# Column sums of the modulation vectors: block turning on VectorE and one small product, in place of eight turns or eight products on TensorE

## What is computed

```python
def _modulation(cvec, w, b):
    m = jax.nn.silu(cvec) @ w + b          # cvec: 2048, w: 2048 x 6144
    return m[..., :D_MODEL], m[..., D_MODEL:2 * D_MODEL], m[..., 2 * D_MODEL:]   # shift, scale, gate
```

## Time and profile before

| | us |
|---|---|
| median of three runs | 2005.06 |
| lowest, highest | 2004.21, 2007.96 |
| span of the profiled execution | 2003.6 |
| TensorE busy, matmuls | 1967.3 (98%), 12638 instructions |
| VectorE busy | 1612.0 (80%), 2209 instructions |
| ScalarE busy | 967.3 (48%) |
| GpSimd busy | 211.4 (11%) |
| HBM read | 430.83 MB |
| granted TensorE clock, mean | 0.995 of full |

### The profile page before, as it was taken

One profiled execution on the slowest core, in us unless ns is written; L12 is line 12 of the kernel. 1 busy time (PEld: TensorE's weight loads), 2 busy tenths in 40 slices (PEclk: granted clock), 3 DMA queues, 4 the chain that ended last, 5 costly groups with the idle time before them and its releaser, 6 DMA issues.

```text
span 2003.6 us, 35002 instructions
## 1 busy us (share of the span) xinstructions
PE 1967.3 (98%) x12638; PEld 1767.2 (88%) x12638; DVE 1612.0 (80%) x2209; ACT 967.3 (48%) x1457; POOL 211.4 (11%) x294
## 2 busy tenths in 40 slices
PE   7999999999999999999999999999999998999997
PEld 7998899899888888888888899887888888999986
DVE  6996677757888998889999878779987877678754
ACT  6553446645444344443444455236565455554453
POOL 0000000011000220001311111111000131000011
PEclk9999999999999999999999999999999999999999
DMA  6554454346777787777888874677657884568553
GB/s 239 168 159 137 159 198 127 106 158 200 231 234 229 265 317 238 237 235 241 286 295 295 305 262 159 228 232 230 211 169 226 273 285 156 193 196 288 189 190 126
DMA packets 121148, 434.43 MB, mean 217 GB/s; under 512 B 13248, under 2 KB 15680, under 8 KB 120784
## 3 DMA queue, kind: packets, MB, share of 16 engines
q1 hardware_dynamic: 92240, 328.11, 49.8%
q0 software_dynamic: 28800, 104.87, 15.8%
HBM read 430.83 MB, written 2.10 MB: 216 GB/s over the span
## 4 chain that ended last, share of the span: by engine, by line
PE 85%; DVE 9%; DMA 3%; issue 2%; ACT 1%; SPq 0%; DVEq 0%; POOL 0%; POOLq 0%; ACTq 0%
PE ps L649 33%; PE ps L650 16%; PE ps L636 7%; PE ps L637 7%; PE ps L638 7%; DVE w_lo L1690 3%; PE ps L784 2%; DMA side<-w_side 2%; PE ps L1108 1%; PE ps L1098 1%; PE ps L717 1%; PE ps L719 1%; PE ps L718 1%; DVE mod_sum L1707 1%; PE ps L826 1%
## 5 line engine op out<-in xcount | busy, mean ns | idle before, releaser
L649 PE MATMUL ps<-ba_act,w_hi 128*128 128x512 f32 x3264 | 1152.4, 398 | 2.6 <-DVE w_lo L1690 2.6
L650 PE MATMUL ps<-ba_act,w_lo 128*128 128x256 f32 x3264 | 910.8, 279 | 0.0
L1690 DVE TENSOR_TENSOR w_lo<-raw,w_hi 128x1024 fp32r<-128x1024 f32 x610 | 728.9, 1236 | 35.1 <-ACT w_hi L1252 34.2
L649 PEld LDWEIGHTS ps<-ba_act,w_hi 128*128 128x128 f32 x3264 | 612.6, 188 | 149.4 <-issue 4.2
L1252 ACT ACTIVATE w_hi<-raw 128x1024 fp32r<-128x1024 f32 x610 | 612.4, 1042 | 222.0 <-PE ps L638 162.1
L650 PEld LDWEIGHTS ps<-ba_act,w_lo 128*128 128x128 f32 x3264 | 615.1, 188 | 1.3 <-issue 1.2
L636 PE MATMUL ps<-ba_act,w_hi 128*128 128x256 f32 x912 | 261.8, 287 | 5.2 <-DVE w_lo L1690 5.1
L637 PE MATMUL ps<-ba_act,w_hi 128*128 128x256 f32 x912 | 258.9, 284 | 0.0
L638 PE MATMUL ps<-ba_act,w_lo 128*128 128x256 f32 x912 | 258.8, 284 | 0.0
L1707 DVE SCALAR_TENSOR_TENSOR mod_sum<-side,csil,mod_sum 128x1024 f32<-128x1024 f32 x180 | 229.0, 1286 | 32.1 <-DMA side<-w_side 28.9
L544 POOL DMA_DIRECT2D side<-w_side x200 | 108.1, 541 | 1350.8 <-DVE mod_sum L1707 770.9
(11 more groups left out here) (368 smaller groups left out, 1860.4 us busy)
## 6 DMA issues: line engine op xcount, KB each, us to landing
raw<-w_main SPq DMA_DIRECT2D x610, 512.0 KB, 4.4
side<-w_side POOLq DMA_DIRECT2D x200, 512.0 KB, 4.6
x_tok<-x_in SPq DMA_DIRECT2D x4, 512.0 KB, 8.0
ctx_tok<-ctx_tok SPq DMA_DIRECT2D x1, 2048.0 KB, 10.6
y_out<-res SPq DMA_DIRECT2D x4, 384.0 KB, 3.1
table<-counts_tab SPq DMA_DIRECT2D x1, 512.0 KB, 12.9
y_out<-res SPq DMA_DIRECT2D x2, 256.0 KB, 3.0
cons<-cons_in SPq DMA_DIRECT2D x1, 478.0 KB, 10.7
```

What stands on the lines that cost most here:

```text
L649: pe.matmul(ps[:, bank, :], wh, act[:, kt, :, :], start=first and b == 0, stop=False)
L650: mm = pe.matmul(ps[:, bank, 0:T], wl, act[:, kt, 0, :], start=False, stop=last and b == 7)
L1690: dve.tensor_tensor(w_lo[:, slot, 0:n], raw[:, slot, 0:n], w_hi[:, slot, 0:n].bitcast(F32), ALU.subtract)\
```

## The change

Of eleven groups (all but `ev_out`) the sum over the partitions is split in two.

- VectorE turns the whole 128 x 1024 sum in one instruction that transposes 32 x 32 blocks, each inside its own 32 partitions and 32 columns, and then adds up each block's 32 columns (`turn_mods`): 128 x 32 remain, `mod_part`, in which the four groups of 32 partitions are still apart. This runs in body 0 of the stage for the first vector, body 1 for the second (one later in `ev_q2` and `ev_z`), and for `od_z` after the first step of `pool`.
- TensorE then multiplies `mod_part` of both vectors in one product with `fold`, a 128 x 128 matrix of sixteen 32 x 32 identities (`fold_mods`). This runs two steps after the last turn (after step 3, or 2 where there is one vector), and for `od_z` after the third step of `pool`.
- VectorE adds the bias and sorts in four small additions of 32 partitions x 8 for each vector, in the body after that.

`fold` takes the place of a constant that nothing used, and is built in step 30 by one reduction of 128 x 128 and one copy. `ev_gate` is made in step 6 of `down2` instead of 2. `ev_out` keeps its products with ones. Five or six first steps of some stages are written out where two or three were. Cut to its core:

```diff
+def turn_step(stage, k):
+    c = k - SUMS_STEP.get(stage, 0)
+    return c if stage in SUMS_OF and 0 <= c < mod_vecs(SUMS_OF[stage]) else None
+
+def fold_step(stage):
+    return SUMS_STEP.get(stage, 0) + 1 + mod_vecs(SUMS_OF[stage])
...
+        mod_part = small("mod_part", [P, 2, BLK])
...
+        turned_both = at("turned_both", PR + 8 * K, [P, 2, HALF])
...
-                    if stage in SUMS_OF and isinstance(i, int):
-                        c = k - SUMS_STEP.get(stage, 0)
-                        if 0 <= c < mod_vecs(SUMS_OF[stage]):
-                            sum_mods(SUMS_OF[stage], c)
+                    if stage in SUMS_OF and isinstance(i, int) and k == fold_step(stage):
+                        fold_mods(SUMS_OF[stage])
...
+            def fold_mods(stage):
+                n = mod_vecs(stage)
+                pe.wait_ge(mods_summed, mod_sums(stage, 1))
+                pe.matmul(ps[:, mod_bank(stage), 0:BLK * n], fold, mod_part[:, 0:n, :], start=True, stop=True)\
+                  .then_inc(mods_summed, 1)
...
-                if g == 0:
-                    sum_mods("od_z", 0)
+                if g == 2:
+                    fold_mods("od_z")
...
+            def turn_mods(stage, c):
+                if c == 0:
+                    dve.wait_ge(mods_added, DT * (MOD_STAGES.index(stage) + 1))
+                turned = turned_of(stage)[c]
+                then(dve.transpose(turned, mods_of(stage)[c]))
+                ins = dve.tensor_reduce(mod_part[:, c, :], turned.rearrange("p (b r) -> p b r", r=BLK), AX.X, ALU.add)
+                if c == mod_vecs(stage) - 1:
+                    ins.then_inc(mods_summed, 1)
+
+            def read_mods(stage):
...
+                dve.wait_ge(mods_summed, mod_sums(stage, 2))
+                for c in range(mod_vecs(stage)):
+                    for g in range(P // BLK):
+                        rows = slice(BLK * g, BLK * (g + 1))
+                        summed = ps[rows, mod_bank(stage), BLK * c:BLK * (c + 1)].rearrange("p (t b) -> p b t", b=4)[:, g, :]
+                        ins = dve.tensor_tensor(mods[rows, t0:t0 + 8, c], summed, col("mod_b", t0, 8)[rows, :], ALU.add)
...
-                        c = k - SUMS_STEP.get(stage, 0) - 1
-                        if 0 <= c < mod_vecs(SUMS_OF[stage]):
-                            read_mods(SUMS_OF[stage], c)
+                        c = turn_step(stage, k)
+                        if c is not None:
+                            turn_mods(SUMS_OF[stage], c)
+                        if k == fold_step(stage) + 1:
+                            read_mods(SUMS_OF[stage])
...
+                        then(dve.tensor_reduce(fold[:, 0:BLK], ident.rearrange("p (b c) -> p c b", c=BLK), AX.X, ALU.add))
+                        dve.tensor_copy(fold[:, BLK:P].rearrange("p (b c) -> p b c", c=BLK), cbc(fold[:, 0:BLK], 3))\
+                           .then_inc(S("n_kg"), 1)
...
+                if g == 0:
+                    turn_mods("od_z", 0)
             read_mods("od_z")
```

More of the change, by code:

```diff
@@ L114, with mod_sums, mod_bank @@
 BOTH = (0, 1, 2, 3)
-MOD_BANK = {"ev_kv": 4, "ev_q": 6, "ev_q2": 6, "ev_out": 7}
+BLK = 32
+ONES_BANK = 7
 def mod_vecs(stage):
     return 2 if MOD_GROUPS[stage] in BOTH else 1
-def mod_sums(stage, c):
-    return sum(mod_vecs(n) for n in MOD_STAGES[:MOD_STAGES.index(stage)]) + c + 1
+def mod_sums(stage, n):
+    return sum(1 if name == "ev_out" else 2 for name in MOD_STAGES[:MOD_STAGES.index(stage)]) + n
+def mod_bank(stage):
+    return 7 if MOD_GROUPS[stage] < 6 else 6
 SUMS_OF = {"down0": "up0", "up1": "down0", "down1": "up1", "up2": "down1", "up2b": "up2", "down2": "up2b",
@@ L453, in vbc @@
             return ap.rearrange("p (w a) -> p w a", a=1).to_broadcast([ap.shape[0], ap.shape[1], n])
-        ident, ones = con("ident"), con("ones")
+        ident, ones, fold = con("ident"), con("ones"), con("rot")
         raw_full = [S(f"raw_full{j}") for j in range(4)]
@@ L478, in mods_of, with turned_of @@
             return [mod_sum[:, g % 2, :]]
+        def turned_of(stage):
+            if MOD_GROUPS[stage] in BOTH:
+                return [turned_both[:, c, :] for c in range(2)]
+            if stage in ("up2", "up2b"):
+                return [turned_up2[:, :]]
+            return [turned_z[:, :] if stage == "ev_z" else turned_ev[:, :]]
         block = stack.enter_context(nc.Block())
@@ L755, in body @@
                         norm_sums(before)
[L756 to L759 removed]
+                    if stage in SUMS_OF and isinstance(i, int) and k == fold_step(stage):
+                        fold_mods(SUMS_OF[stage])
                 steps(pe, stage, body,
[L761 removed]
+                      first=COUNT[stage] if chain is not None else 4 if stage in SUMS_OF else 2 if split else 0)
                 if summed is not None and sums:
@@ L778, in body @@
                         next(chain)
-                    if stage in SUMS_OF and k == SUMS_STEP.get(stage, 0):
-                        sum_mods(SUMS_OF[stage], 0)
+                    if stage in SUMS_OF and k == fold_step(stage):
+                        fold_mods(SUMS_OF[stage])
                 steps(pe, stage, body, first=COUNT[stage] if chain is not None else 2 if reads is not None else 0)
@@ L784, in turn, with sum_by_ones @@
                 return pe.transpose(ps[0:ncols, bank, at_col:at_col + rows], src_ap, ident[base:base + rows, base:base + rows])
-            def sum_mods(stage, c):
+            def fold_mods(stage):
[3 more added lines that the diff above has]
+                  .then_inc(mods_summed, 1)
+            def sum_by_ones(stage):
                 g = MOD_STAGES.index(stage)
                 pe.wait_ge(mods_added, DT * (g + 1))
-                summed = mods_of(stage)[c]
+                summed = mods_of(stage)[0]
                 for t in range(8):
[L792 to L796, removed]
+                    mm = pe.matmul(ps[:, ONES_BANK, t:t + 1], summed[:, t * P:(t + 1) * P], ones[:, 0:1], start=True, stop=True)
                 mm.then_inc(mods_summed, 1)
@@ L1749, in reading @@
                 if grouped:
-                    first = COUNT[stage] if COUNT[stage] != DT else max(first, 3)
+                    first = COUNT[stage] if COUNT[stage] != DT else max(first, 6 if stage in SUMS_OF else 3)
                 steps(dve, stage, body, first=COUNT[stage] if chain is not None else first)
```

31 lines of the change are left out of this document (14 added, 17 removed).

## The result

The changed kernel takes **2015.8 us** in the median of 7 runs (2012.17 to 2018.71), the kernel before 2005.18 beside it (7 runs): ratio 1.0048, interval 1.0037 to 1.0059. It is 10.6 us slower, where 0.7 was forecast. By the prediction's own line (4 us tells a measurement from no change) this is "slower", to which it gave 0.29, and not "same", to which it gave 0.50. Its range of 1999 to 2016 still holds the median, by 0.2 us. A second set of 5 runs gave 2013.74 us beside 2005.94, 7.8 slower, and 1.0045 (1.003 to 1.006). The profiled execution is a long one: 2018.19 us, its span 2016.5.

What follows compares the result with a forecast made beforehand. The prediction took TensorE and VectorE as both full in `down1`. Feed-forward +5.5, attention -4.6, `ev_out` -0.6 and pooling +0.4 gave +0.7 us, so 2005.06 + 0.7 = 2005.8 us, range 1999 to 2016.

Steps and rivals of the forecast that it cites:

- signs: Expected in the profile after: TensorE stops of 1 to 3 us in feed-forward stages; wrong if it stops in attention stages.
- The turn: VectorE's transpose of the whole sum: 1.2 us per vector, 2.40 with the reduction.
- Both rivals on the turn: VectorE's transpose takes 2.42 us at half rate (2019 us, chance 0.15), or a fast 0.75 us (2001 us, chance 0.10).
- The fold: TensorE's eleven new products: 0.25 us each, 2.75 us in all.
- Stops where the spare ends: Feed-forward stages: TensorE waits where VectorE's lateness exceeds its lead above 1.61 us (spare); these stages end 5.5 us later.
- Burst absorbed: Rival: in the feed-forward stages the spare is larger, TensorE keeps its 13.2 us; 1992 us, chance 0.08.
- The small additions: VectorE's four small additions per vector: 0.08 us each, 0.33 for four.
- down0: Stage `down0`: VectorE late 2.99 us against a spare of 3.02, so no TensorE stop; 0.25 us later with the fold.
- D: TensorE's lateness against the old trace, carried through the feed-forward stages: from 0.25 us after `down0` to 5.5 after `down2`.
- The attention part: `ev_q`, `ev_q2` and `ev_z` win 4.6 us together, since VectorE's extra 2.7 us fit its free time; `ev_out` wins 0.63.
- attention eats the gain: Rival: VectorE's extra 2.7 us hold up the softmax chain in the attention stages, losing the 4.6; 2010.4 us, chance 0.13.
- `pool` and `od_out`: `pool` stops 0.65 us and gets a fold, `od_out` starts 1.0 us sooner; +0.4 us taken as lost.

Runs made afterwards that it cites:

- turns_kept: Changed kernel with TensorE's 80 old turns in the feed-forward stages put back as load that nobody reads: 2015.44 us, ratio 1.0057.
- one_addition: Changed kernel with one addition of 128 partitions in place of four of 32 per feed-forward vector (values misplaced): 2013.64 us, ratio 1.0035.
- no_turn_in_feed_forward: Changed kernel without the ten VectorE turns of the feed-forward stages (those modulation vectors are wrong): 2003.32 us, ratio 0.999.
- after_again: The changed kernel unaltered, measured and traced once more: 2013.74 us, span 2006.9.
- down0_group_alone: Kernel before with only the group of `down0`, summed in `up1`, done the new way: 2006.31 us, ratio 1.0013.

## Why the range held, and why the sum was too small

The range of 1999 to 2016 held by luck. Its upper part was put there for a turn at half rate, and the turn came out as forecast. The forecast's own range, 2002 to 2009, missed. What was right is the direction in each half and most of the mechanism; what was wrong is the size in the feed-forward stages, +11 to +15 us against +5.5. Of the signs, TensorE did stop in an attention stage (`ev_q`, 1.24 and 1.98 us, where before had 0.86 and 1.74), and VectorE is busy for 97% of `down0` and over 99% of `down1`.

- **The turn: right.** 1.23 to 1.24 us, 2.40 with the reduction, as taken. The Trainium skill, page "Vector Engine (DVE) Microarchitecture Reference", section 3.8, with one element per cycle and lane, agrees: the turn's row (1.24) is the reduction's (1.22) within 2%. The 311 ns that the Trainium skill, page "VectorE: DVE Perf Modes", section "The three transpose paths", gives for 128x128 in bf16 don't scale to this width: eight of them would be twice the row. Both rivals on the turn fall.
- **The fold: right.** In step 3 of `down0` the two L681 on either side of it start at 673.65 and 674.23, 0.58 apart, where 0.35 is usual: 0.23; 0.25 was taken.
- **Stops where the spare ends, and the old turns no gain: right.** They stand at step 3 of `up1`, `down1` and `up2`, and turns_kept shows the 1.76 lost each time. In `up2b` the forecast stop is missing: I gave the stage +0.7, and both traces (69.9 and 70.6) lie between the two of before (69.1 and 70.7); `down2` has stops at its first steps. Together the two stages are 1.9 and 1.7 us longer, 1.4 forecast. "Burst absorbed" falls.
- **The small additions: term mis-sized.** 0.33 for four was taken from an addition of 128 partitions; those of 32 take 0.71. Whether that is their width isn't shown: each of the four also starts in another group of 32 partitions than the one ahead of it, and their rows don't overlap. one_addition puts the term at 2 us at most in the time.
- **down0: the step that failed.** I tested its step 3 and gave the stage 0.25; it got 2.0 and 2.3. At step 3 TensorE was 0.2 ahead of the old trace (668.45 - 650.01 from the stage's start, against 668.92 - 650.31). But I had noted for `down1` that the eight additions and a saturated VectorE make a second stop at step 6, and didn't carry it to `down0`, which is as full: 686.22, 0.76 us. In one_addition, without the extra small additions, that stop is gone. By step 15 the stage is 1.0 behind.
- **Lateness that I let vanish at a stage's end.** The other 1.0 lies at the first product of `up1`: it waits 1.32 us where it waited 0.29 (before):

```profile
742.63 0.47 PE L649 MATMUL ps<-ba_act,w_hi 128*128 128x512 f32 x1 [0.29 <-DVE w_lo L1690]
```

  I took only D over into the next stage, as though VectorE's own lateness within its spare cost nothing. But the slot of a half is freed by VectorE, and SP's loads wait for that. Timelines of SP and of ScalarE ahead of `up1`, before:

```profile
728.28 15.90 SPq L503 DMA_DIRECT2D raw<-w_main  x6
...
740.16 2.26 ACT L1252 ACTIVATE w_hi<-raw 128x1024 fp32r<-128x1024 f32 x2 [2.97 <-DMA raw<-w_main]
```

and after:

```profile
730.64 15.27 SPq L534 DMA_DIRECT2D raw<-w_main  x6
...
741.87 1.06 ACT L1285 ACTIVATE w_hi<-raw 128x1024 fp32r<-128x1024 f32 x1 [4.00 <-DMA raw<-w_main]
```

  The loads are issued 2.4 us later, so `w_hi` comes 1.7 later, and with it `w_lo`. The load that this first product needs takes 11.8 us to land before and 10.8 after. The same place also limits the gain: in no_turn_in_feed_forward it takes 11.5, TensorE gets there early and stops 2.2 us.
- **Two terms missing altogether.** The new way brings the 5.65 tempo into stages that ran at 5.55, by its stops or its folds: in `down1` alone 16 steps by 0.106 (45.22 - 44.37, by 8) are 1.7 us, and in `up1` of the first trace, nearly all of it slow, 3.3 of its 5.5. And the stretches at 1.2 GHz: three in the feed-forward stages of the first trace, 1.5 us for each of the two shown, and one in `ev_q`. The terms can't simply be added, since a slower TensorE stops less. They can make up most of the 6.3 us between the stage sums of the two traces of one program. In the second trace, without such stretches and with `up1` at its old tempo, the stages are still 11.2 longer: 5.5 forecast, about 3 tempo in `down1` and `up2`, 2 in `down0`.
- **The attention part: right in size, a part of it left to chance.** 3.9 for `ev_q2`, `ev_z` and `ev_out` against 3.7 forecast; `ev_q` between -2.0 and +1.4 against -1.5. The rival "attention eats the gain" is true of `ev_q` in most traces, by a mechanism it didn't name: not the chain's lateness alone, but, as the traces with and without a stretch suggest, the clock behind its stops. `pool` and `od_out` cancel; +0.4 was taken.

What stays open: what decides between the two tempos, and which stops are followed by 1.2 GHz. That the slow tempo comes with the new way rests on `down1` in fourteen traces, of which thirteen agree, and not on a run that set it; one of the thirteen has no stop there, only the fold. So the steps that failed in `down0` and at the start of `up1` are shown. The two missing terms are measured, but their causes are open.

## What to carry to other kernels

When work moves from TensorE to an engine that paces it, what TensorE gives up isn't a gain: count what the pacing engine gets, stage by stage, against its idle time in that stage. Carry an engine's whole lateness into the next stage, through the buffers it frees, not only the part beyond its spare. And price a stop at more than its length: it may lower the clock behind it. The half of the change that lay where VectorE had free time was worth keeping alone: 2000.13 us against 2005.94, while the whole costs 8 to 11 us.

## What the runs showed of the hardware

- An addition of 32 partitions x 8, each in another group of 32 than the one ahead of it, takes 0.18 us to the next on VectorE, one of 128 partitions x 8 takes 0.08.
- A 32x32-block turn of 128x1024 float32 takes 1.24 us, the same as a reduction of as much (1.22).
- The same products at the same granted clock run at 5.55 or 5.65 us a step, for stretches of up to hundreds of us, and change mostly at interruptions (after and before, `down1`; after and after_again, `up1`).
- A stop can be followed by 1.2 GHz: 1.93 us was (after, `up1`), 1.35 us was (down0_group_alone, `ev_q`), 1.86 us wasn't (after_again, `up2`).
- A `w_lo` takes 1.22 us, but 1.75 to 2.06 in some 30 of 610 cases, and each of these runs beside work of GpSimd. In the kernel before the second `w_lo` of a step in `down1` takes 1.76 us (the one at 937.38, beside the one of GpSimd): this is a part of why VectorE has no free time there.
